# A hybrid encoder layer with a 32-expert MoE: gathering the next expert's rows between gate's and up's products, and scattering in two parts

## What is computed

```
logits = xt @ w_router + b_router            # 256 x 32
top_val, top_idx = top_k(logits, 4); wts = softmax(top_val)
for each expert e, for the rows routed to it:
    g = x @ w_gate[e] + b_gate[e]            # 1024 x 1024 each
    u = x @ w_up[e]   + b_up[e]
    g = min(g, 7); u = clip(u, -7, 7)
    act = (u + 1) * g * sigmoid(1.702 * g)
    y = act @ w_down[e] + b_down[e]
    out[row's token] += weight * y
```

## Time and profile before

| what | value |
|---|---|
| median of 3 runs | 1543.1 us (1540.38 to 1544.27) |
| the profiled execution | 1546.29 us, its span 1544.3 us, mean granted clock 0.984 |
| PE matmul busy | 1460.4 us, 95% of the span |
| DVE, ACT, POOL busy | 619.2, 391.3, 151.7 us |
| HBM read over the span | 489.72 MB, 318 GB/s |

### The profile page before, as it was taken

One profiled execution on the slowest core, in us unless ns is written; L12 is line 12 of the kernel. 1 busy time (PEld: TensorE's weight loads), 2 busy tenths in 40 slices (PEclk: granted clock), 3 DMA queues, 4 the chain that ended last, 5 costly groups with the idle time before them and its releaser, 6 DMA issues.

```text
span 1544.3 us, 18679 instructions
## 1 busy us (share of the span) xinstructions
PE 1460.4 (95%) x7595; PEld 849.2 (55%) x7595; DVE 619.2 (40%) x1118; ACT 391.3 (25%) x570; POOL 151.7 (10%) x91
## 2 busy tenths in 40 slices
PE   6978997899999999999999999999999999999998
PEld 6876776777778877444444443433433433443343
DVE  5896569777775585212122221211211111112112
ACT  5435455545545443010010100100100100100010
POOL 4245322111111220000000000000000000000000
PEclk9999999999999997999999999999999999999999
DMA  7334334445444685899999999999999999999996
GB/s 243 114 132 150 104 115 136 144 154 163 144 146 177 237 323 220 334 428 427 429 428 429 429 428 428 429 429 428 428 429 429 429 428 428 429 429 428 428 429 265
DMA packets 72651, 491.39 MB, mean 318 GB/s; under 512 B 5168, under 2 KB 7344, under 8 KB 48032
## 3 DMA queue, kind: packets, MB, share of 16 engines
q1 hardware_dynamic: 69648, 487.76, 78.1%
q10 hardware_dynamic: 2448, 2.62, 0.6%
q0 software_dynamic: 512, 0.43, 0.1%
HBM read 489.72 MB, written 1.07 MB: 318 GB/s over the span
## 4 chain that ended last, share of the span: by engine, by line
PE 63%; DMA 23%; DVE 9%; ACT 2%; issue 2%; POOL 1%; DVEq 0%; SPq 0%; ACTq 0%
DMA regions<-in_w_up 22%; PE ps L1674 18%; PE ps L1712 10%; PE ps L1382 6%; PE ps L1383 6%; PE ps L1384 6%; PE ps L1605 5%; PE ps L1369 3%; PE ps L1650 3%; DVE splits L931 1%; DVE regions L1034 1%; DVE regions L1032 1%; ACT splits L673 1%; PE ps L1540 1%; DVE regions L950 1%
## 5 line engine op out<-in xcount | busy, mean ns | idle before, releaser
L1674 PE MATMUL ps<-regions,sig 128*64 128x512 f32 x2048 | 463.4, 597 | 25.9 <-DMA regions<-in_w_up 25.0
L1674 PEld LDWEIGHTS ps<-regions,sig 128*64 128x64 f32 x2048 | 142.1, 137 | 322.2 <-issue 263.1
L1382 PE MATMUL ps<-splits,regions_r 128*128 128x512 f32 x512 | 215.4, 421 | 11.9 <-DVE splits L931 9.2
L1712 PE MATMUL ps<-regions,tmp 128*64 128x512 f32 x1024 | 225.1, 592 | 0.0
L1383 PE MATMUL ps<-splits,regions_r 128*128 128x512 f32 x512 | 202.7, 396 | 0.0
L1384 PE MATMUL ps<-splits,regions_r 128*128 128x512 f32 x512 | 202.6, 396 | 0.0
L673 ACT ACTIVATE splits<-halves 128x1024 fp32r<-128x1024 f32 x152 | 158.7, 1054 | 107.4 <-PE ps L1384 96.9
L931 DVE TENSOR_TENSOR splits<-halves,splits 128x1024 fp32r<-128x1024 f32 x114 | 142.3, 1256 | 69.9 <-ACT splits L673 69.2
L831 ACT ACTIVATE work<-work 128x512 f32<-128x512 f32 x32 | 20.2, 630 | 528.3 <-DVE work L1327 528.3
L1712 PEld LDWEIGHTS ps<-regions,tmp 128*64 128x64 f32 x1024 | 71.9, 137 | 131.8 <-issue 129.4
L580 POOL TENSOR_TENSOR splits<-halves,splits 128x1024 fp32r<-128x1024 f32 x38 | 93.2, 2451 | 424.0 <-ACT splits L673 424.0
(11 more groups left out here) (243 smaller groups left out, 1346.4 us busy)
## 6 DMA issues: line engine op xcount, KB each, us to landing
regions<-in_w_gate SPq DMA_DIRECT2D x64, 2048.0 KB, 30.1
regions<-in_w_up SPq DMA_DIRECT2D x64, 2048.0 KB, 33.2
regions<-in_w_down SPq DMA_DIRECT2D x64, 2048.0 KB, 35.4
halves<-in_w_in SPq DMA_DIRECT2D x48, 1024.0 KB, 5.2
halves<-in_w_br_b SPq DMA_DIRECT2D x8, 1024.0 KB, 5.1
halves<-in_w_mem_kv SPq DMA_DIRECT2D x8, 1024.0 KB, 5.1
halves<-in_w_br_a SPq DMA_DIRECT2D x4, 1024.0 KB, 5.1
halves<-in_w_br_c SPq DMA_DIRECT2D x4, 1024.0 KB, 6.9
```

Source lines behind the costliest of these rows:

```text
L1382: pe.matmul(out, lhs[0], rhs[0], start=start, stop=False, skip_group_check=True)
L1674: last = pe.matmul(ps[64 * h:64 * h + 64, bank, :], xgT[:, k % 2 * 4 + c], eslots[slot][:, c, h * NB:(h + 1) * NB], start=(k % 2 == 0 and ...
L1712: last = pe.matmul(ps[64 * h:64 * h + 64, D_BANK, :], actT[:, c, 64 * k:64 * k + 64], eslots[slot][:, c, h * NB:(h + 1) * NB], start=False ...
```

## The change

- `xgT` becomes two buffers, used in turn by the parity of the expert.
- `gather()` of expert i + 1 is issued by PE after gate 1's matmuls and ahead of up 0's. DVE's `take_gathered` moves from behind the activation to between g times sigmoid and the clamp of u.
- The scatter is cut in two: `scatter(0)` (the first 128 tokens, 4 matmuls) ahead of the four transposes of the activation, `scatter(1)` (the other 128 tokens) behind them.
- The two transposes of `hot_w` move behind `scatter(1)` and go to `U_BANK`; ACT's copy of them moves behind its copy of `actT`. The wait for it (`scatter_ready`) is now at up's first matmul and at the next `scatter(0)`, no longer at down.

```
-                    act.wait_ge(sem("hot_wT_ready"), i + 1)
-                    act.activation(hot_wT, ps[:, D_BANK, 0:T]...).then_inc(sem("scatter_ready"), 1)
                     act.wait_ge(sem("actT_out"), i + 1)
                     act.activation(actT..., ps[:, G_BANK, :], ACT.Copy).then_inc(sem("actT_ready"), 1)
+                    act.wait_ge(sem("hot_wT_ready"), i + 1)
+                    act.activation(hot_wT, ps[:, U_BANK, 0:T]...).then_inc(sem("scatter_ready"), 1)
...
                         dve.tensor_tensor(gu_sb, g_sb, sg_sb, ALU.mult).then_inc(sem("gu_ready"), 1)
+                        take_gathered(i + 2, (r + 1) % 2)
...
-                        take_gathered(i + 2)
...
+                            if k == 2:
+                                pe.wait_ge(sem("scatter_ready"), i + 1)
...
-                                    last = pe.matmul(ps[64 * h:64 * h + 64, bank, :], xgT[:, k % 2 * 4 + c],
+                                    last = pe.matmul(ps[64 * h:64 * h + 64, bank, :], xgT[r % 2][:, k % 2 * 4 + c],
...
-                        scatter(i)
-
-                        pe.wait_ge(sem("hot_w_ready"), i * TT + TT)
-                        for t in range(TT):
-                            last = turn(ps[:, D_BANK, t * P:(t + 1) * P], hot_w[:, t]...)
-                        last.then_inc(sem("hot_wT_ready"), 1)
+                            if k == 1:
+                                pe.wait_ge(sem("hot_ready"), i * TT + 2 * TT)
+                                gather()
+                        pe.wait_ge(sem("yb_ready"), i + 1)
+                        pe.wait_ge(sem("scatter_ready"), i + 1)
+                        scatter(0)
                         pe.wait_ge(sem("act_ready"), i + 1)
                         for c in range(4):
                             last = turn(ps[:, G_BANK, c * P:(c + 1) * P], act_sb[:, c * P:(c + 1) * P])
                         last.then_inc(sem("actT_out"), 1)
-                        pe.wait_ge(sem("hot_ready"), i * TT + 2 * TT)
-                        gather()
+                        scatter(1)
+                        pe.wait_ge(sem("hot_w_ready"), i * TT + TT)
+                        for t in range(TT):
+                            last = turn(ps[:, U_BANK, t * P:(t + 1) * P], hot_w[:, t]...)
+                        last.then_inc(sem("hot_wT_ready"), 1)
                         pe.wait_ge(sem("actT_ready"), i + 1)
-                        pe.wait_ge(sem("scatter_ready"), i + 1)
```

More of the change, by code:

```diff
@@ L360, in hybrid_block_kernel @@
         act_sb, actT = tmp[:, 0], tmp[:, 1].rearrange("p (c j) -> p c j", c=4)
-        yb, xgT = sig[:, 0], sig[:, 1].rearrange("p (c j) -> p c j", c=KC)
+        yb = sig[:, 0]
+        xgT = [sig[:, 1].rearrange("p (c j) -> p c j", c=KC), S[:, 1, 0:NB].rearrange("p (c j) -> p c j", c=KC)]
         spare = craw[:].rearrange("p a b t -> p (a b t)")
@@ L622, in _ @@
                     pool.memset(qz, 0.0).then_inc(sem("qz_zero"), 1)
-            pool.memset(hot_wT, 0.0).then_inc(sem("hot_wT_zero"), 1)
+            pool.memset(hot_wT, 0.0).then_inc(sem("scatter_ready"), 1)
         @block.scalar
@@ L831, in _ @@
                     act.activation(sg_sb, g_sb, ACT.Sigmoid, scale=ALPHA).then_inc(sem("sg_ready"), 1)
-                    act.wait_ge(sem("hot_wT_ready"), i + 1)
-                    act.activation(hot_wT, ps[:, D_BANK, 0:T].rearrange("p (t j) -> p t j", t=TT),
-                                   ACT.Copy).then_inc(sem("scatter_ready"), 1)
                     act.wait_ge(sem("actT_out"), i + 1)
@@ L837, in _ @@
                         .then_inc(sem("actT_ready"), 1)
+                    act.wait_ge(sem("hot_wT_ready"), i + 1)
+                    act.activation(hot_wT, ps[:, U_BANK, 0:T].rearrange("p (t j) -> p t j", t=TT),
+                                   ACT.Copy).then_inc(sem("scatter_ready"), 1)
         @block.vector
@@ L1257, in find, with take_gathered @@
                         .then_inc(sem("hot_ready"), 1)
-            def take_gathered(n):
+            def take_gathered(n, buffer):
                 dve.wait_ge(sem("gather_ready"), n)
-                dve.tensor_tensor(xgT, ps[:, X_BANK, :].rearrange("p (c j) -> p c j", c=KC),
+                dve.tensor_tensor(xgT[buffer], ps[:, X_BANK, :].rearrange("p (c j) -> p c j", c=KC),
                                   gain2_rows[:].unsqueeze(2).to_broadcast([P, KC, BLK]), ALU.mult)\
@@ L1284, in _ @@
             dve.tensor_copy(npass_i[:], npass_f[0:1, :]).then_inc(sem("passes_known"), 1)
-            take_gathered(1)
+            take_gathered(1, 0)
             dve.memset(yb, 0.0).then_inc(sem("yb_ready"), 1)
@@ L1642, in _, with scatter @@
             gather(1, 2)
-            def scatter(n, signal=None):
-                pe.wait_ge(sem("yb_ready"), n + 1)
-                for t in range(TT):
[L1648 to L1655, removed]
+            def scatter(t, signal=None):
+                for h in range(2):
+                    rows = slice(64 * h, 64 * h + 64)
+                    last = pe.matmul(ps[:, ACC[2 * t + h], :], hot_wT[rows, t], yb[rows], start=False, stop=False,
+                                     skip_group_check=True)
+                    if signal is not None:
+                        last.then_inc(signal, 1)
+                return last
             pe.wait_ge(misc_taken, MISC_END)
@@ L1685, in _ @@
                                               start=False, stop=False, skip_group_check=True)
-                        scatter(i)
-                        pe.wait_ge(sem("hot_w_ready"), i * TT + TT)
-                        for t in range(TT):
-                            last = turn(ps[:, D_BANK, t * P:(t + 1) * P], hot_w[:, t].rearrange("p r j -> p (r j)"))
-                        last.then_inc(sem("hot_wT_ready"), 1)
+                            if k == 1:
[4 more added lines that the diff above has]
+                        scatter(0)
                         pe.wait_ge(sem("act_ready"), i + 1)
@@ L1696, in _ @@
                         last.then_inc(sem("actT_out"), 1)
-                        pe.wait_ge(sem("hot_ready"), i * TT + 2 * TT)
-                        gather()
+                        scatter(1)
+                        pe.wait_ge(sem("hot_w_ready"), i * TT + TT)
+                        for t in range(TT):
+                            last = turn(ps[:, U_BANK, t * P:(t + 1) * P], hot_w[:, t].rearrange("p r j -> p (r j)"))
+                        last.then_inc(sem("hot_wT_ready"), 1)
                         pe.wait_ge(sem("actT_ready"), i + 1)
-                        pe.wait_ge(sem("scatter_ready"), i + 1)
                         for h in range(2):
@@ L1715, in _ @@
                             last.then_inc(e_used[slot], 1)
-            scatter(n_pass * EXPERTS, sem("sums_ready"))
+            pe.wait_ge(sem("yb_ready"), n_pass * EXPERTS + 1)
+            pe.wait_ge(sem("scatter_ready"), n_pass * EXPERTS + 1)
+            for t in range(TT):
+                scatter(t, sem("sums_ready"))
 def kernel(**inputs):
```

## The result

The change makes the kernel slower: 1560.51 us median of four runs (1551.71 to 1563.22) against 1542.39 for the kernel before, now of four runs too (1540.38 to 1544.27), a ratio of **1.0103, 95% interval 1.0077 to 1.0129**. 1560 was forecast, in a range of 1546 to 1568.

A forecast was written before the change was run, and what follows sets the result against it. Loads at 29.36 us an expert bound the kernel before; after the change PE, at 27.62 + 3.83 + 3.98 - 6.25 = 29.18, sets the end. Down ends 16.3 us later, giving 1560 us, range 1546 to 1568.

The forecast's parts named there:

- The bound before: Kernel before: PE needs 27.62 us an expert, loads 29.36; PE catches up, then waits in about the last 20 experts.
- The leg from up's end to down's bias: PE's stretch with scatter and transposes in each expert: 3.98 us after the change, including a 0.9 us stall, against 6.25 before.
- The gather: Between gate 1 and up 0 in each expert: the moved gather with its changes of array shape adds 3.83 us.
- The period: PE's time per expert after the change: 27.62 + 3.83 + 3.98 - 6.25 = 29.18 us, under the loads' 29.36.
- The sum: Whole span: down ends at 1553.5 instead of 1537.24, +16.3 us, as PE never catches up with the loads.
- The tie at P = 28.70: Expert 31's last up: at a PE period of 28.70 us, PE and the loads set the end equally.
- the tail at 11.23: PE's work behind the last up, to down's end: 11.23 us after the change, 13.50 before.
- the 0.71 us of the bounds: Upper bound: added changes of array shape at twice their price cost 0.71 us more, P = 29.9 and 1582 us.
- Loads pace the end: Rival: loads still set the end if P is under 28.7; 1542 to 1543 us, no change; chance 0.15.
- PE behind the loads too: Rival: P above 29.36 through slower waking or dearer shape changes; P of 29.4 gives 1567 us; past 1568, chance 0.10.
- The gather's place pays: Rival: the gather fills PE's idle ahead of up's loads, shortening the tail by 3.6 us; something better, chance 0.03.

The follow-up runs named there:

- e7: The kernel before with every load from the ninth half on fetching half its bytes; 1508.44 us, ratio 0.9773 to the kernel before.
- e5: The kernel before with hot_w's two transposes moved between the scatter's two halves; ratio 1.0005 to the kernel before.
- e3: The changed kernel with scatter(1) directly behind scatter(0), so the scatter is whole again; ratio 0.9999 to the kernel before.
- e1: The kernel before with only the gather moved between gate 1 and up 0, with two buffers and take_gathered moved; ratio 1.0012 to the kernel before.
- e2: The changed kernel with the gather and take_gathered back in their old places, scatter still split; ratio 1.0048 to the kernel before.
- e6: The kernel of e3 with the gather moved between gate 0 and gate 1; ratio 0.9987 to the kernel before.
- e4: The changed kernel with hot_w's two transposes put between scatter(0) and the activation's transposes; ratio 1.0051 to the kernel before.

## Why the prediction was right, point by point

- **The bound before.** Two regimes, PE at 27.62 and the loads at 29.36 us an expert. e7 shows it: with the loads halved the period stays 27.62 and 33 us go. The place where PE catches up, about the last 20 experts, was right too: the first period longer than 27.62 is the twelfth.
- **The leg from up's end to down's bias.** 3.98 forecast, 3.97 measured. The stall is 0.83 us in PE's row, from the fourth matmul's modelled end; from `scatter(0)`'s 1.06 to the transposes' start at 1.96 it is 0.90. PE reacts 0.05 behind DVE, as estimated (1542.23 + 1.07 to 1543.35 in the chain).
- **The gather.** 3.83 forecast, 3.86 measured: leaving gate's shape 0.09, the gather 3.72 to up's start, and up's first pair takes 0.05 more than 0.43. The gather was forecast at 3.67 (3.61 and 0.06), from its place behind the transposes, which have its shape. The change from column pairs to the full array, which no row of before showed, cost what the others did. e5 measures two changes alone at 0.35; the Trainium skill's sentence on changing the tiling mode (TensorEngine Tiling (Array Packing), Key Properties) agrees with these costs, 0.09 for leaving and 0.05 to 0.10 for entering.
- **The period.** 29.18 forecast, 29.22 measured, over 31 experts 1.2 us.
- **The sum.** The forecast said +16.3 us on the profiled span, and it came to 15.5: 1.2 more for the period, 2.4 less because the experts began at 614.53 rather than 616.94, and 0.4 of small ends. The experts alone, from their first matmul to down's end, took 17.8 us longer. That the median came within 1 us of the forecast is luck: the runs themselves spread over 11.5.
- **Two figures beside the sum.** The tie at P = 28.70 leaves out the 3.83 us that the moved gather adds once, ahead of expert 0's up; with it, and with the tail at 11.23, down's end ties at (1537.24 - 11.23 - 637.71) / 31 = 28.65. And the 0.71 us of the bounds counts an entry of 0.06 that the kernel before has as well: only the four added changes free give about 28.54 rather than 28.47. Neither moves the forecast.
- **Where the gain of the moves went.** The change does fill time and does shorten the tail, by 2.3 us. But the idle that it fills, PE's wait for up's loads, existed only because the loads were late, and what it adds, 1.6 us an expert, is more than the 1.0 to 1.1 that could be hidden there.
- **The rivals.** Loads pace the end: false for the change, true for e3 and e5, with the threshold where it was put: a period of 28.72 (e1) still costs nothing measurable, 28.88 (e2) costs 7.4 us and 29.22 (the change, ratio 1.0103) costs 16. The Trainium skill's rule to improve the most-contended engine (Perfetto Trace Analysis, Identifying Performance Opportunities) would have named DMA here. The traces agree for the kernel before, late in the run, where PE waits for loads at 428 GB/s; in the changed kernel DMA moves the same 428 GB/s and PE waits for none. PE behind the loads too: didn't occur. The gather's place pays: by itself no (e1); behind gate 0 with a whole scatter the kernel is 0.13% faster (e6), and only the traces put that down to the place.

The forecasts of e1 to e5 were 0.5 to 2 us low: by their ratios e1, e2, e4 and e5 came out at +1.8, +7.4, +7.9 and +0.8 us where +0.6, +6.7, +6 and +0.3 were expected, and e3 at -0.2 where -1 was, each inside its interval. For e1 the period explains most of it: 28.72 instead of the expected 28.69 makes 0.9 us over 31 experts. By the experts' part of the traces, measured as above, e1 takes 1.8 us more than before, e2 7.0, e3 1.0, e4 6.6 and e5 1.2. Whether the rest is noise or a small cost of the early experts, where up's slots are released later, wasn't settled.

## What to carry to other kernels

When two resources are both near full, compare their periods per iteration, not their shares. The slower one hides what is added to the faster up to a limit, and past it every 0.1 us counts once per iteration. Where the faster one starts behind and has to catch up, as here, the limit is less than the difference of the periods: 1.1 us instead of 1.74. Before work is moved to fill one gap, look at which latency it covers where it stands; here the scatter was as long as DVE's activation, and the gather covered ACT's copy. And putting work of another shape into the middle of a group of packed matmuls costs a change of shape on each side of it, 0.35 us together in e5.

## What the runs showed that was not expected

The kernel's runs spread with the mean granted clock: of 31 runs of the kernel before on one chip, the five at 0.983 and 0.984 took 1545.8 to 1546.6 us, and those at 0.990, 0.991 and 0.992 took 1538.05, 1535.71 and 1534.55. The changed kernel's four runs follow the same line, from 0.984 with 1563.22 to 0.993 with 1551.71. In the profile of before the longest stretch at the 1.2 GHz level comes as the experts begin: the granted clock is 0.50 from 605 to 620 us, after PE had been busy for 48.0 of the 50 us up to 600, and 1.00 from 625 us on. By the figures above, 1% of mean clock goes with 13 to 15 us on either kernel, more than most of the changes tried here. In the traces most of this spread lies ahead of the experts, which begin between 609.76 us (e4) and 616.94 (before). A median of four runs carries it, and the experts' periods, read from one trace, don't: while nothing but PE paces them, they agree within 0.02 us in the kernel before and in the changed one.
